# First attention of a two-block kernel: scores over all 128 rows of the array, values one step later

## The reference

```
q, k: [tokens, 8, 2, 64]   v: [tokens, 8, 128]
o1 = softmax(q[..., 0, :] @ k[..., 0, :].T / 8) @ v
o2 = softmax(q[..., 1, :] @ k[..., 1, :].T / 8) @ v
o  = o1 - lam * o2
o  = rms_norm(o, subln_g) * (1 - lam_init), then o * silu(z), then @ w_out
```

## Time and profile before

| | us |
|---|---|
| median of 3 runs | 780.48 (780.07 to 780.59) |
| the profiled execution | 780.35 |
| its span, first to last instruction | 778.3 |
| TensorE busy | 765.4 (98%) |
| VectorE busy | 550.9 (71%) |
| ScalarE busy | 392.4 (50%) |
| GpSimd busy | 42.5 (5%) |
| granted TensorE clock, mean | 1.00 |

### The profile page before, as it was taken

One profiled execution on the slowest core, in us unless ns is written; L12 is line 12 of the kernel. 1 busy time (PEld: TensorE's weight loads), 2 busy tenths in 40 slices (PEclk: granted clock), 3 DMA queues, 4 the chain that ended last, 5 costly groups with the idle time before them and its releaser, 6 DMA issues.

```text
span 778.3 us, 11220 instructions
## 1 busy us (share of the span) xinstructions
PE 765.4 (98%) x4137; PEld 613.8 (79%) x4137; DVE 550.9 (71%) x985; ACT 392.4 (50%) x749; POOL 42.5 (5%) x55
## 2 busy tenths in 40 slices
PE   8999999999999999999999999999999999999998
PEld 6668777887777788867788888787788888888886
DVE  3456998987677867599757766998977554555553
ACT  4452222328788765566656656625444444444441
POOL 0120000000001010112100002200100000000000
PEclk9999999999999999999999999999999999999999
DMA  9995554333000085249222055963325855665621
GB/s 325 361 379 191 207 216 167 116 121 137 2 1 1 1 314 209 71 152 340 76 92 74 6 175 166 365 221 107 100 69 183 270 163 164 204 209 182 203 67 55
DMA packets 72409, 125.78 MB, mean 162 GB/s; under 512 B 2842, under 2 KB 36844, under 8 KB 71204
## 3 DMA queue, kind: packets, MB, share of 16 engines
q1 hardware_dynamic: 71504, 123.00, 45.9%
q10 hardware_dynamic: 388, 1.08, 0.4%
q0 software_dynamic: 464, 0.98, 0.4%
HBM read 123.99 MB, written 1.06 MB: 161 GB/s over the span
## 4 chain that ended last, share of the span: by engine, by line
PE 73%; DVE 16%; ACT 3%; DMA 3%; issue 2%; SPq 1%; POOL 1%; DVEq 0%; ACTq 0%
PE psum L871 15%; PE psum L873 14%; PE psum L872 14%; DVE w_lo L2004 5%; PE psum L1067 3%; PE psum L1092 3%; PE psum L1388 3%; PE psum L1387 3%; PE psum L1386 3%; PE psum L993 2%; PE psum L860 2%; PE psum L1165 2%; PE psum L861 2%; PE psum L862 2%; DMA kT<-in_ada_w 2%
## 5 line engine op out<-in xcount | busy, mean ns | idle before, releaser
L872 PE MATMUL psum<-w_lo,act_hi 128*128 128x512 f32 (+1 forms) x624 | 242.1, 388 | 0.0
L871 PE MATMUL psum<-w_hi,act_hi 128*128 128x512 f32 (+1 forms) x584 | 237.4, 407 | 2.9 <-DVE act_lo L2187 2.5
L873 PE MATMUL psum<-w_hi,act_lo 128*128 128x512 f32 (+1 forms) x584 | 226.9, 388 | 0.0
L2004 DVE TENSOR_TENSOR w_lo<-raw,w_hi 128x2048 fp32r<-128x2048 f32 (+1 forms) x68 | 153.2, 2261 | 62.3 <-ACT w_hi L1425 62.3
L1425 ACT ACTIVATE w_hi<-raw 128x2048 fp32r<-128x2048 f32 (+1 forms) x72 | 136.2, 1894 | 67.5 <-PE psum L873 30.9
L871 PEld LDWEIGHTS psum<-w_hi,act_hi 128*128 128x128 f32 x584 | 109.7, 188 | 37.7 <-issue 13.5
L872 PEld LDWEIGHTS psum<-w_lo,act_hi 128*128 128x128 f32 x624 | 117.5, 188 | 20.4 <-issue 0.5
L873 PEld LDWEIGHTS psum<-w_hi,act_lo 128*128 128x128 f32 x584 | 109.6, 188 | 23.3
L1973 POOL TENSOR_TENSOR rstd<-ms,half_neg 128x1 f32<-128x1 f32 (+3 forms) x38 | 36.0, 950 | 521.5 <-DVE ms L2045 521.5
L860 PE MATMUL psum<-act_hi,w_hi 128*128 128x512 f32 x128 | 50.7, 396 | 1.7 <-DVE w_lo L2004 1.7
L861 PE MATMUL psum<-act_lo,w_hi 128*128 128x512 f32 x128 | 50.0, 390 | 0.0
(11 more groups left out here) (295 smaller groups left out, 1123.0 us busy)
## 6 DMA issues: line engine op xcount, KB each, us to landing
raw<-in_a_w_in SPq DMA_DIRECT2D x16, 1024.0 KB, 8.7
raw<-in_ada_w SPq DMA_DIRECT2D x14, 1024.0 KB, 5.1
raw<-in_w_out SPq DMA_DIRECT2D x12, 1024.0 KB, 5.4
raw<-in_w_gate SPq DMA_DIRECT2D x22, 512.0 KB, 4.2
raw<-in_w_up SPq DMA_DIRECT2D x22, 512.0 KB, 5.3
raw<-in_w_down SPq DMA_DIRECT2D x11, 1024.0 KB, 4.9
raw<-in_b_w_in SPq DMA_DIRECT2D x10, 1024.0 KB, 7.5
raw<-in_w_in SPq DMA_DIRECT2D x10, 1024.0 KB, 6.0
```

The source lines that it names most:

```text
L871: pe.matmul(oh, x_hi, hi, start=(k == 0), stop=False)
L872: pe.matmul(o[:, 0:n], x_hi, lo, start=False, stop=False)
L873: mm = pe.matmul(oh, x_lo, hi, start=False, stop=(k == KT - 1))
L2004: ins = dve.tensor_tensor(rest, weights, hi.bitcast(F32), ALU.subtract)
```

## The change

The scores are computed over all 128 rows. For that the halves of the keys are exchanged: `round_k[:, h, :]` keeps the rounded first half in partitions 0 to 63 and gets the rest of the first half in 64 to 127; `rest_k[:, h, :]` gets the rounded second half in the low partitions and keeps its rest in the high ones. The low and high halves of the stationary operand hold the same query twice. A matmul over 128 rows with the rounded query then gives q_hi x k_hi + q_hi x k_lo, and one with the query's rest adds q_lo x k_hi + q_lo x k_lo. So each s takes 2 matmuls instead of 3, each over 128 rows.

SyncE does the exchange and the doubling by transfers from SBUF to SBUF. `exchange(pair)` handles two heads: 2 transfers of 128 KB into the buffer `taken`, a wait, 2 transfers, a wait, 2 transfers, and for all but the last pair of heads a wait. `doubled_queries(pair)` copies the queries of two steps: 8 transfers of 64 KB, in pieces of 512 bytes, into one slot of the `w_lo` ring, two generations deep. An entry "doubled" in the load plan holds that slot, and later loads shift by one.

The values of a step move one step back: in step p TensorE does the transposes of p, the values of p - 1, the scores of p + 2, then the gate's piece. ScalarE's `move` of t0(p) goes ahead of `beside0(p - 1)` and `out0(p - 1)`.

```diff
+EXCHANGED_BEFORE = {("in0", 6, 0): [0, 1], ("doubled", 0, 0): [2], ("in0", 7, 0): [3]}
+DOUBLED_BEFORE = {("in0", 7, 1): [2], ("out0", 0, 0): [3], ("out0", 0, 1): range(4, 9), ("out0", 1, 0): range(9, 16)}
...
+            def exchange(pair):
+                heads = slice(2 * pair, 2 * pair + 2)
+                last = HEADS + 2 * pair + 1
+                b, at = place[("in0", BY_FEATURES[0] + last // NT, last % NT)]
+                sp.wait_ge(s_rest0, last + 1)
+                sp.wait_ge(free[b], at + 1)
+                aside = taken[:].rearrange("p t n -> p (t n)").bitcast(F32)
+                for i, half in enumerate((LOW, HIGH)):
+                    sp.dma_start(aside[half], round_k[HIGH, 2 * pair + i, :].bitcast(F32)).then_inc(s_exchanged, 16)
+                sp.wait_ge(s_exchanged, 96 * pair + 32)
+                for h in (2 * pair, 2 * pair + 1):
+                    sp.dma_start(round_k[HIGH, h, :].bitcast(F32), rest_k[LOW, h, :].bitcast(F32)).then_inc(s_exchanged, 16)
+                sp.wait_ge(s_exchanged, 96 * pair + 64)
+                for i, half in enumerate((LOW, HIGH)):
+                    sp.dma_start(rest_k[LOW, 2 * pair + i, :].bitcast(F32), aside[half]).then_inc(s_exchanged, 16)
+                if pair < HALF_KT - 1:
+                    sp.wait_ge(s_exchanged, 96 * pair + 96)
...
+            def doubled_queries(pair):
+                t, h = STEPS0[2 * pair]
+                if pair == 0:
+                    sp.wait_ge(s_rest0, HEADS)
+                elif pair >= 2:
+                    b, at = place[("s0", 2 * pair - 3, 1)]
+                    sp.wait_ge(full[b], at + 1)
+                r = slice(2 * (pair % 2), 2 * (pair % 2) + 2)
...
+                for s, own in enumerate((LOW, HIGH)):
+                    for half in (LOW, HIGH):
+                        sp.dma_start(doubled[half, s, r, 0, :].bitcast(F32), tokens[own]).then_inc(s_doubled[pair % 2], 16)
+                        sp.dma_start(doubled[half, s, r, 1, :].bitcast(F32), rests[own]).then_inc(s_doubled[pair % 2], 16)
...
+                for pair in EXCHANGED_BEFORE.get(loads[n], ()):
+                    exchange(pair)
+                if loads[n][0] == "doubled":
+                    sp.wait_ge(*emptied[n - RAW])
+                    for pair in range(2):
+                        doubled_queries(pair)
+                    continue
+                for pair in DOUBLED_BEFORE.get(loads[n], ()):
+                    doubled_queries(pair)
...
@@ scores0 (TensorE)
-                o = [begin(("s0", p, s)) for s in range(2)]
-                for i in range(3):
-                    for s in range(2):
-                        rows = slice(64 * s, 64 * s + 64)
-                        q = rest_q[rows, p, :] if i == 2 else round_q[rows, h, tile_cols(t)]
-                        k = (rest_k if i == 1 else round_k)[rows, h, keys]
-                        mm = pe.matmul(o[s][:, 0:n], q, k, start=(i == 0), stop=(i == 2))
...
+                pe.wait_ge(s_doubled[p // 2 % 2], 128 * (p // 4 + 1))
+                pe.wait_ge(s_exchanged, 96 * (h // 2 + 1))
+                for s in range(2):
+                    o = begin(("s0", p, s))
+                    k = (round_k, rest_k)[s][:, h, keys]
+                    for i in range(2):
+                        mm = pe.matmul(o[:, 0:n], doubled[:, s, p % 4, i, :], k, start=(i == 0), stop=(i == 1))
+                    mm.then_inc(bank_full(("s0", p, s)), 1)
...
@@ the 32 steps (TensorE)
                 turn_probs(("t0", p), sc[:, 4 + p % 2, :], XT if STEPS0[p][0] >= XT else NT)
+                if p:
+                    values0(p - 1)
                 if p + 2 < NT * HEADS:
                     scores0(p + 2)
...
-                values0(p)
...
@@ the 32 steps (ScalarE)
+                n = XT * P if STEPS0[p][0] >= XT else NT * P
+                move(sc[:, 6 + p % 2, 0:n], ("t0", p), n=n, wait_for=("pv0", p - 2) if p >= 2 else None)
                 if p:
                     beside0(p - 1)
                     out0(p - 1)
-                n = XT * P if STEPS0[p][0] >= XT else NT * P
-                move(sc[:, 6 + p % 2, 0:n], ("t0", p), n=n, wait_for=("pv0", p - 2) if p >= 2 else None)
```

More of the change, by code:

```diff
@@ L90, in loads_plan @@
             plan += both("ada0g", 1)
+        elif c == 6:
+            plan.append(("doubled", 0, 0))
     for stage, chunks in (("out0", 2), ("in1", 5), ("out1", 2), ("in2", 6), ("out2", 2)):
@@ L302, in block_kernel @@
     load_no = {key: n for n, key in enumerate(loads)}
-    halves = [key for key in loads if not key[0].startswith("ada")]
+    halves = [key for key in loads if not key[0].startswith("ada") and key[0] != "doubled"]
     half_no = {key: g for g, key in enumerate(halves)}
@@ L450, in block_kernel @@
         s_gatein = sem("first_gate_chunk_in")
+        s_exchanged = sem("key_halves_exchanged")
+        s_doubled = [sem(f"doubled_queries{i}") for i in range(2)]
         N_CIN, N_VEC, N_LATE = 3, 4, 10
@@ L582, in block_kernel @@
         for n, (stage, c, h) in enumerate(loads):
-            n_landed[n % RAW] += 32 if stage == "gu" else 16
+            n_landed[n % RAW] += 32 if stage == "gu" else 0 if stage == "doubled" else 16
             landed_at[n] = n_landed[n % RAW]
@@ L588, in block_kernel @@
         for n, (stage, c, h) in enumerate(loads):
-            if stage == "ada0g":
+            if stage == "doubled":
+                b, at = place[("s0", NT * HEADS - 1, 1)]
+                emptied[n] = (full[b], at + 1)
+            elif stage == "ada0g":
                 emptied[n] = (s_sumused, h + 1)
@@ L619, in bank @@
             return psum[:, place[name][0], 0:n]
+        LOW, HIGH = slice(0, 64), slice(64, P)
+        doubled_at = load_no[("doubled", 0, 0)] % RAW
+        doubled = w_lo[:, doubled_at, :].rearrange("p (s r i n) -> p s r i n", s=2, r=4, i=2)
         block = ctx.enter_context(nc.Block())
@@ L648, in modulation @@
                         sp.dma_start(ada0_bufs[n][:, :, w * 2 * P:(w + 1) * 2 * P], src).then_inc(ada0_landed[n], 16)
+            def exchange(pair):
[23 more added lines that the diff above has]
+                r = slice(2 * (pair % 2), 2 * (pair % 2) + 2)
+                tokens = round_q[:, h, :].rearrange("p (s t n) -> p s t n", s=2, t=XT)[:, :, t, :].bitcast(F32)
+                rests = rest_q[:, 2 * pair:2 * pair + 2, :].bitcast(F32)
+                for s, own in enumerate((LOW, HIGH)):
+                    for half in (LOW, HIGH):
+                        sp.dma_start(doubled[half, s, r, 0, :].bitcast(F32), tokens[own]).then_inc(s_doubled[pair % 2], 16)
+                        sp.dma_start(doubled[half, s, r, 1, :].bitcast(F32), rests[own]).then_inc(s_doubled[pair % 2], 16)
             load(silu_t[0:8, 0, :], a["c"].rearrange("a (k p) -> (a k) p", p=P), s_cin)
@@ L1105, in _ @@
                         pe.wait_ge(*moved(("in0", 5 * (p // 8), t)))
-                values0(p)
                 if p in (24, 26):
                     to_feature("turn_o0", [0], gate_units, parts=((p - 24) // 2,))
+            values0(NT * HEADS - 1)
             to_feature("turn_o0", [2], gate_units)
```

2 lines of the change are left out of this document (removed).

## The result

The changed kernel takes 800.78 us (median of 4 runs, 799.82 to 801.26) beside 780.54 (780.07 to 780.93) for the kernel before: ratio 1.0257, 95% interval 1.0244 to 1.0269. The prediction said slower, at 783.7 and at most 788; the loss is 20.2 us where it had 3.2. In the profiled execution (799.82) the span is 797.9 us against 778.3.

A forecast was written before the change was run, and what follows sets the result against it. The prediction took TensorE, busy 98% of the span, to bound the kernel, with the loop feeding it taking back its saving. It summed 780.48 + 2.7 (steps) + 0.5 (transfers) = 783.7 us, range 776.0 to 788.0 for 8 in 10.

The forecast's parts named there:

- The transfers: SyncE's exchanges and doublings: the start costs 0 to 2 us, taken as +0.5; later pairs are hidden, cost 0.
- The loop that feeds it: Scores, maximum, exponentials, combination, transposes: in the new order TensorE waits, making a four-step cycle 0.40 us longer.
- the light wait: Before the light transposes behind each tanh, once a cycle: TensorE waits 0.94 us for VectorE's combination.
- A cycle is 12.26: TensorE's own work in four attention steps: 12.26 us against 13.21, 0.95 less, if nothing waits.
- The border: Time lost around the old 64-row score matmuls on TensorE: 0.41 us a step, gone after the change.
- The waits before heavy transposes: TensorE waiting for the combination before heavy steps of a cycle: 0.31 us in one, 0.18 in another.
- The first steps have none and gain 0.4: The first attention steps, before the cycles with the tanh: no waits for it, a gain of 0.4 us.
- Sum of the steps: +2.7: All 32 attention steps: +2.8 us from seven cycles, +0.3 from weight rounding, 0.4 gained in the first steps.
- TensorE-bound: Rival on the attention loop: the combination comes in time and TensorE's saving shows, 773.4 us; chance 0.18.
- The change doesn't do what it says: Rival on the scores: the 0.41 us a step is their semaphore waits and stays, 786.6 us; chance 0.05.
- Doubled queries late: Rival on the doubling transfers: late at the start or in every pair, 14 x 0.7 us, 793 us; chance 0.08.
- What would show it: Trace signs: no 64-row matmul, cycle about 13.6, light waits near 0.9, heavy 0.2 to 0.3; wrong if TensorE awaits transfers.

The follow-up runs named there:

- 11: The changed kernel with only the exchanges moved from SyncE's queue to GpSimd's, doubled queries staying on SyncE: 787.58 us, ratio 1.0092.
- 1: The kernel before with only the two moves in the order of work (values one step later, ScalarE's move of t0 ahead of tanh and out0): 787.68 us.
- 2: The changed kernel without exchange and doubling, scores of the new form read from the data as they lie: 787.23 us, ratio 1.0082.
- 4: The changed kernel with 30 matmuls whose results nobody reads ahead of the first scores, keeping TensorE awake: 800.76 us, ratio 1.0257.
- 9: The changed kernel with exchanges on GpSimd, doublings placed earlier, and VectorE's gate product behind the next odd step's combination and maximum: 783.77 us, ratio 1.0041.
- 10: New scores, TensorE's old order, exchanges on GpSimd, earlier doublings, VectorE's gate product later, ScalarE's tanh behind the move of t0, out0 ahead: 777.94 us, ratio 0.9968.
- 3: The changed kernel without exchange and doubling, with the old order on TensorE and ScalarE, so the new scores alone: 778.71 us, ratio 0.9977.
- 6: The kernel before with one edit, ScalarE's move of t0 ahead of tanh and out0, TensorE's order untouched: 789.43 us, ratio 1.0114.
- 5: The changed kernel without exchange and doubling, with ScalarE's move of t0 put back behind tanh and out0, TensorE's new order kept: 782.21 us, ratio 1.0019.

## Why the prediction was right in sign and wrong in size

The 20.2 us come out of two measured pieces: exchanges on SyncE's queue 13.2 (the changed kernel less 11), and the rest 7.0 (11 less the kernel before). Of this rest the order of work is 7.1 alone (1), the new form of the scores -0.5 beside it (2 less 1), and the transfers that are left 0.35 (11 less 2).

**The step that failed is "The transfers".** It said: "Issuing costs about 0.4 each", "I expect it to end near 164", "Cost of the start: 0 to 2, I take +0.5", later pairs "hidden", exchanges 0 and 1 "cost 0, bounds 0 and 1". In its place:

- Pair 0's issues start at 169.59, not at 163.3 when the ring slot comes free: 6.3 late. Exchange 2 holds SyncE for 5.4 of it (in 11, without it, they start at 164.19). I let it end near 164, three short rounds behind the load at 153.16. In fact exchange 1 runs on to 154.70 and moves both 1 MB loads there, exchange 2 begins at 155.72 right behind them, and its first round takes 8.2 instead of 2.8.
- The eight issues take 5.6 us to the end of the last (169.59 to 175.15) against 3.2: 2.4 more. The rows that I had the earlier trace rows are of loads of another shape, in a pair; 0.4 was a price for an operation that the trace did not hold, and I gave it no second end. My landing at 168.5 becomes 177.2 with 6.3 and 2.4; the first scores start at 176.65, 7.2 us after TensorE ran dry.
- Pair 2 was never followed. The text gave later pairs the time from slot release to use, and left out what stands between them on SyncE: exchange 3, 181.03 to 187.9, and a load. It costs the second wait, 1.95 us; in 4, where TensorE came to it 2.1 us earlier, the same wait was 4.13.

The order from the kernel's table, written out as a line of SyncE's issues with three dependent round trips for each exchange, would have put both in sight, though no row before had the length of a round behind loads. The estimate in that step by the Trainium skill ("DMA: Bandwidth & Descriptors", Anatomy of one DMA, which gives the fixed 2 us and the 436 GB/s for DMAs that GpSimd issues) was 3.2 us a pair. The trace has a landing of 2.1 us (median of 64) for one of the eight, near that fixed part, but a pair takes 5.2 (8 x 0.65) for the issue alone: what sets the pace is SyncE.

**"The loop that feeds it" held in its mechanism.** The tanh behind the move of t0, once a cycle, is the cause of the light wait, which is gone in 9. I followed the cycle from step 12 (231.00). There the combination's chain begins at +2.42 (2.36 worked out), the combination ends at 234.40, and the transposes see it at +3.46 (3.43). TensorE would have been ready 0.23 after the start of its last gate matmul (233.33), at +2.56 (2.49). So from start to start it waits 0.90, where I had 0.94; the timeline, which counts from the end of a record, says 0.73. The hand-over of 0.08 was right too (0.06). The 0.93 of step 9 looks like a better match and is none: 0.20 of it comes after the usual hand-over, from something else. TensorE has four more semaphore waits at the end of step 8 (`if p in (0, 8)`), for moves done long before; that they cost the 0.20 was not tested. Two terms were mis-sized:

- "A cycle is 12.26": in the new order it is some 12.5 where nothing waits. The cycle of 12.67 in 9 has two waits of 0.1 before heavy transposes that no PE row lists (the last gate matmul 0.34 and 0.32 ahead of them instead of 0.23), and from step 8 to 12 the changed kernel has the same, 13.79 less 1.09 before step 9 and 0.10 and 0.13 before steps 10 and 12. Heavy scores take 1.02 (218.07 to 219.09), not 0.92, light ones 0.55 (221.93 to 222.48), not 0.47. The border does go, as predicted, but the saving in TensorE's own time is some 0.7 a cycle, not 0.95. The extra 0.1 lies between the first and the second matmul of the scores (0.31 from 219.43 to 219.74 in 2, where the next follow 0.23 or 0.24 apart). It is not the two added semaphore waits, since 2 has neither: my 0 for these was right.
- The waits before heavy transposes, for which I had 0.31 and 0.18: the cycles are not alike. From step 4 on they take 13.83, 13.79, 14.41, 14.55, 14.10 and 14.40 us, where before has 13.36, 13.21, 13.22, 13.21, 13.21 and 14.12 (starts of the transposes of steps 4, 8, ..., 28). Up to step 12 the heavy waits come to 0.2 to 0.5 a cycle, from start to start; before steps 14 and 16 they are 0.24 and 0.76, before 18 and 20 0.39 and 0.76. The roundings on ScalarE at steps 14 and 18 stand there, for which I had 0.3 in all; that they are the whole cause was not tested. Six cycles together are 4.75 us longer, not 2.4 and 0.3.

"The first steps have none and gain 0.4" failed as well: in 2 the transposes of step 4 are 1.1 late. "Sum of the steps: +2.7" is thus 6.7 (2), a factor of 2.5. The rest of the distance is the transfers.

**The rivals.** TensorE-bound: its time, 773.4, was not reached by any kernel. The best one (10) has a cycle of 12.34 from step 8 to 12 (203.60 to 215.94), near my 12.26 though in the old order on TensorE, but the six cycles from step 4 take 78.25 us in all, 13.04 on average: most of the border's worth goes into cycles that something other than TensorE sets. "The change doesn't do what it says" falls by 3 and by the neighbours in the rows at 218.07: no 64-row matmul, no border. This is also the case for which the Trainium skill ("TensorEngine Tiling (Array Packing)", When to Use Tiling) advises row tiles; here four full passes beat three packed ones, by 1.9 us over 32 steps (3). "Doubled queries late" had the right place, a chance of 0.08 and 9.8 us where the transfers cost 13.6; but it priced each pair as bandwidth, 14 x 0.7, when it is a queue at the start, twice, so that its 793 is the nearest of my times for another reason.

**"What would show it"** answered well where it was precise: L2405 waits longer, light waits are close to 0.9 from start to start; heavy ones reach 0.76, not 0.2 to 0.3; "SyncE's 8 issues near 0.4 each, TensorE's first scores within 1 us of 169.4" both failed, and with them "wrong if it waits for transfers" came true.

**What stays open.** Why ScalarE's move alone (6, 8.8 us) costs more than both moves (1, 7.1): the row of `qT` points to the bank that the values need (all steps' values use the same one, bank 7), but this was not tested by a kernel of its own. What sets the 0.61 us of a doubling transfer. What lengthens the cycles behind step 12. And whether the tanh or the output is the greater part of the 5.0 us in 5; 9, where the product that waits for the tanh is out of the way, gives back 2.7.

## What to carry to other kernels

Write out an in-order issuing queue as a timetable before you call its transfers hidden: a chain of transfer, wait, transfer holds everything behind it, and here each round that followed two 1 MB loads paid for them (8.2 and 9.4 us instead of 2.8). Such a chain belongs on an engine that nobody waits behind; here one such edit was worth 13.2 of 20.2 us. When an order is rotated on two engines at once, follow every instruction that is passed over (the tanh, the output) to its reader, since an engine that is half idle can still set the cycle.

## What the hardware showed that I had not expected

A DMA of 64 KB in 512-byte pieces from SBUF to SBUF holds SyncE for 0.61 us (median of 64, 0.59 to 1.44), one of 128 KB in an exchange 0.46 to 0.63, a 1 MB load from HBM 0.37 in the kernel before, and 0.60 here at 193.81, between two pairs. The times from issue to landing of the exchanges' first rounds (the line's answer: count, shortest, median and longest issue in ns):

```profile
L677 SPq DMA_DIRECT2D taken<-round_k x8: 462/566/628, 131.1 to 181.6; - x8
DMA to landing us min/median/max: 2.2/5.0/8.9
```

The second rounds, of the same size, land in 2.2 to 2.3; only first rounds have 1 MB loads just ahead of them, those of exchanges 0 and 2. And behind the wait of 7.2 us TensorE ran at 1.2 GHz for 6 us, in which matmuls of 512 columns started 0.43 us apart instead of 0.23, at no net cost (4), because the next wait was for transfers that did not depend on TensorE. The wait of 1.95, with one of 1.00 shortly ahead of it (before 193.26), was followed by the half clock as well, for 3.2 us. The one of 2.11 in 11, straight behind dense work, was not: the granted clock stays at 1.00.
